# The opening of a two-layer trunk on one core: modulation tiles shared out anew, x loaded in halves, squares added by VectorE, gate dots one place later

## What is computed

```python
m  = (silu(c)     @ w_mod[i] + b_mod[i]).reshape(Bsz, 1, 9, 1024)      # latents
mc = (silu(c_ctx) @ w_mod[i] + b_mod[i]).reshape(1, 1, 9, 1024)        # context
def _modulate(h, g, m, k):
    return rms_norm(h, g) * (1 + m[:, :, 3*k + 1]) + m[:, :, 3*k]
def _half_ffn(h, g, m, k, w1, w3, w2):
    y = (silu(_modulate(h,g,m,k) @ w1) * (_modulate(h,g,m,k) @ w3)) @ w2
    return h + 0.5 * m[:, :, 3*k + 2] * y
# layer 0: half ffn -> attention | SSD -> half ffn; layer 1: half ffn -> RG-LRU | differential attention -> half ffn
```

## Time and profile before

| what | us |
|---|---|
| median of 3 runs (lowest, highest) | 2777.78 (2777.18, 2779.23) |
| the profiled execution, its own time | 2772.38 |
| its span, first to last instruction | 2770.5 |
| TensorE matmul busy in it | 2674.9 (97%) |
| VectorE busy | 2055.8 (74%) |
| ScalarE busy | 1172.4 (42%) |
| GpSimd busy | 390.4 (14%) |

### The profile page before, as it was taken

The page is one execution under the profiler, slowest core; times in us unless marked ns, Lnnn a source line. Parts: engine busy times, 40 slices in busy tenths (PEclk is TensorE's granted clock), DMA queues, the critical chain, the costliest instruction groups (busy, mean ns, idle before and its releaser), DMA issues.

```text
span 2770.5 us, 40128 instructions
## 1 busy us (share of the span) xinstructions
PE 2674.9 (97%) x15624; PEld 2513.8 (91%) x15624; DVE 2055.8 (74%) x3186; ACT 1172.4 (42%) x1855; POOL 390.4 (14%) x312
## 2 busy tenths in 40 slices
PE   5999999999998999999999999999999989999999
PEld 5999999998986799999999999999998875878998
DVE  7887878774558687877777878787888667666674
ACT  3233332446447644332323524232436867534342
POOL 3111111110012521111111211100011420211000
PEclk8999999999999999999999999999999999999999
DMA  9888989611120037889898479884522110378553
GB/s 346 213 236 244 281 251 272 156 65 61 54 68 2 1 123 201 240 240 266 243 268 223 138 214 252 240 240 135 166 76 82 54 61 1 114 197 236 154 163 126
DMA packets 161690, 464.13 MB, mean 168 GB/s; under 512 B 13280, under 2 KB 14432, under 8 KB 160608
## 3 DMA queue, kind: packets, MB, share of 16 engines
q1 hardware_dynamic: 87200, 247.65, 26.1%
q0 software_dynamic: 56448, 146.81, 24.4%
q10 hardware_dynamic: 17856, 67.12, 6.9%
HBM read 459.43 MB, written 148.90 MB: 220 GB/s over the span
## 4 chain that ended last, share of the span: by engine, by line
PE 81%; DVE 10%; DMA 4%; issue 2%; ACT 2%; POOL 0%; ACTq 0%; SPq 0%; DVEq 0%; POOLq 0%
PE banks L698 11%; PE banks L786 11%; PE banks L700 11%; PE banks L702 11%; PE banks L788 11%; PE banks L787 10%; PE banks L705 3%; PE banks L709 3%; PE banks L707 3%; DMA raw<-sums 2%; DVE banks L2028 1%; DVE tmp L2301 1%; PE banks L1233 1%; DVE wl L2023 1%; PE banks L1072 1%
## 5 line engine op out<-in xcount | busy, mean ns | idle before, releaser
L1372 ACT ACTIVATE wh<-raw 128x1024 fp32r<-128x1024 f32 (+2 forms) x194 | 181.7, 937 | 616.6 <-PE banks L702 459.9
L2028 DVE SCALAR_TENSOR_TENSOR banks<-mraw,scb 128x1024 f32<-128x1024 f32 x240 | 304.5, 1269 | 12.9 <-DMA mraw<-in_wmn 9.1
L2023 DVE TENSOR_TENSOR wl<-raw,wh 128x1024 fp32r<-128x1024 f32 (+2 forms) x216 | 234.8, 1087 | 93.5 <-ACT wh L1372 91.2
L1437 ACT ACTIVATE wh<-raw 128x512 fp32r<-128x512 f32 (+1 forms) x210 | 161.5, 774 | 320.9 <-DMA raw<-sums 153.8
L698 PE MATMUL banks<-hh,wh 128*128 128x384 f32 x1056 | 271.3, 338 | 9.9 <-DVE wl L2023 9.7
L700 PE MATMUL banks<-hl,wh 128*128 128x384 f32 x1056 | 270.0, 336 | 0.0
L702 PE MATMUL banks<-hh,wl 128*128 128x384 f32 x1056 | 269.8, 336 | 0.0
L786 PE MATMUL banks<-xh,wh 128*128 128x384 f32 (+1 forms) x796 | 258.5, 325 | 5.0 <-DVE wl L2095 4.8
L788 PE MATMUL banks<-xh,wl 128*128 128x384 f32 (+1 forms) x796 | 257.1, 323 | 0.0
L787 PE MATMUL banks<-xl,wh 128*128 128x384 f32 (+1 forms) x796 | 257.1, 323 | 0.0
L698 PE MATMUL banks<-xh,wh 128*128 128x384 f32 x880 | 231.1, 343 | 21.5 <-DVE xl L2293 12.1
(11 more groups left out here) (426 smaller groups left out, 6276.6 us busy)
## 6 DMA issues: line engine op xcount, KB each, us to landing
raw<-sums SPq DMA_DIRECT2D x140, 512.0 KB, 5.9
sums<-in_w POOLq DMA_DIRECT2D x88, 768.0 KB, 8.5
mraw<-in_wmn ACTq DMA_DIRECT2D x120, 512.0 KB, 5.3
a<-in_w SPq DMA_DIRECT2D x70, 512.0 KB, 4.3
sums<-in_w POOLq DMA_DIRECT2D x22, 1536.0 KB, 9.1
sums<-sums POOLq DMA_DIRECT2D x44, 768.0 KB, 9.5
raw<-in_w SPq DMA_DIRECT2D x80, 384.0 KB, 4.3
raw<-in_w SPq DMA_DIRECT2D x52, 512.0 KB, 3.7
```

The costliest lines, as they stand in the source:

```text
L1372: act.activation(wh[slot][:, 0:nk * P], raw[slot][:, 0:nk * P], ACT.Copy).then_inc(hi_done, 1)
L1437: act.activation(W_HI[slot_of(name, last)], W_SRC[name], ACT.Copy).then_inc(w_hi, 1)
L2023: dve.tensor_tensor(wl[slot][:, 0:nk * P], raw[slot][:, 0:nk * P], wh[slot][:, 0:nk * P].bitcast(F32), ALU.subtract).then_inc(lo_done, 1)
L2028: return dve.scalar_tensor_tensor(B67[:], tile, 1.0, scv[:, s, :], ALU.mult, ALU.mult, accum_out=out)
```

## The change

Tiles, loads and squares of the opening are dealt out anew, and three later places follow from it.

- TensorE takes eight mini tiles (8 to 11 of the scale, 0, 1, 4 and 5 of the shift), VectorE eight (12 to 15, and 2, 3, 6, 7). SP loads scale tiles first; the first two raw weight tiles come right behind `par`; `x` comes in two halves, each behind a group of mini tiles.
- The eight squares go to eight separate buffers (`squares`), VectorE adds them (seven additions, `add_square`), and TensorE sums `ssq` alone. GpSimd only waits for the last mini tile before it starts `weight_sums`.
- VectorE's dots on tiles 6 and 7 stand inside the first norm, behind the first four scaled chunks; the biases of the shift are added in two batches (`shift_batch`), on which ScalarE's `xh` waits.
- Gate tiles are loaded behind the weights of up-chunk 1 (`load_gate_minis`), their dots use `scb0` and stand one place later: behind chunk 0, ahead of and behind chunk 1, ahead of chunk 2. ScalarE's Silu of `scb` moves to up-chunk 1.
- The two `mraw` tiles of up-chunk 2 move to the down places j = 5 of rounds 1 and 2, which then have two tiles each.

```diff
-PE_MINI = (1, 3, 5, 7, 9, 11, 13)
-DVE_MINI = (0, 2, 4, 6, 8, 10, 12, 14, 15)
-MINI_GROUPS = ((0, 1, 2), (3, 4, 5, 6), (7, 8, 9, 10), (11, 12, 13), (14, 15))
+PE_MINI = (8, 9, 10, 11, 0, 1, 4, 5)
+DVE_MINI = (12, 13, 14, 15, 2, 3, 6, 7)
+MINI_GROUPS = ((8, 9, 12), (10, 11, 13), (14, 15), (0, 2), (1, 3), (4, 6), (5,), (7,))
...
         if f == 0:
-            place["down", 1, 2] = place["down", 2, 2] = 2
+            place["up", 2] = 0
+            place["down", 1, 2] = place["down", 2, 2] = place["down", 1, 5] = place["down", 2, 5] = 2
...
+        squares = [ssq, sq[0], sq[1], tmp[0], tmp[1], tmp[2], tmp[3], rstd]
...
+                        if (f, g, i) == (0, 0, 1):
+                            load_gate_minis()
...
+            def load_gate_minis():
+                for q in range(2):
+                    sp.wait_ge(mini_mm, 2 + q)
+                    sp.wait_ge(mini_dot, (13, 18)[q])
+                    sp.dma_start(gmini[q][:], dr["wmn"][16 + 4 * q:20 + 4 * q].rearrange("t p n -> p t n")).then_inc(gmini_landed, 16)
...
             def norm_sums(n, segs):
                 pe.wait_ge(ssq_acc, 7 * (n + 1))
+                if n == 0:
+                    for a, b, _s in segs:
+                        mm = pe.matmul(NP[:, a:b], cst("ones"), ssq[:, a:b], start=True, stop=True)
+                    mm.then_inc(norm_sum, 1)
+                    return
...
             for j in PE_MINI:
-                if j == 11:
-                    pe.wait_ge(con_landed, 16)
+                if j == 0:
+                    pe.wait_ge(x_landed[0], 32)
                     norm_sums(0, SEGS)
-
+                if j == 4:
+                    pe.wait_ge(rstd_ready, 1)
...
-                        if 0 < f < 3 and ch == 1:
-                            take_scb(f + 2, scb)
+                        if f < 3 and ch == 1:
+                            take_scb(f + 2 if f else 1, scb)
...
+            act.wait_ge(par_landed, 16)
+            act.activation(sc[:].rearrange("p k s -> p (k s)"), pr("cc"), ACT.Silu).then_inc(sc_ready, 1)
+            split_hi(0, 0, 0, KC)
+            split_hi(1, 1, 0, KC)
             act.wait_ge(scb_landed, 16)
             act.activation(scb0[:], scb0[:], ACT.Silu).then_inc(scb_ready, 1)
-            act.wait_ge(par_landed, 16)
-            act.activation(sc[:].rearrange("p k s -> p (k s)"), pr("cc"), ACT.Silu).then_inc(sc_ready, 1)
-            act.wait_ge(x_landed, 16)
             for j in range(KC):
-                square(j, 0, x[:, j, :], T)
-            split_hi(0, 0, 0, KC)
-            split_hi(1, 1, 0, KC)
-            act.wait_ge(eps_set, 1)
+                if j % 4 == 0:
+                    act.wait_ge(x_landed[j // 4], (32, 16)[j // 4])
+                act.activation(squares[j][:], x[:, j, :], ACT.Square).then_inc(sq_done, 1)
             norm(0, SEGS, lambda j: None)
             load_scb(scb)
-            take_scb(1, scb)
             ffn(0, KC, 1, T, T)
...
                         def ahead():
+                            if f == 0 and 1 <= ch < 3:
+                                gate_dots(2 * ch - 1)
+                            if f < 3:
+                                dot_mods(f, ("up", ch))
+
+                        def behind():
                             if f == 0 and ch < 2:
                                 gate_dots(2 * ch)
-                            if f < 3:
-                                dot_mods(f, ("up", ch))
-
-                        def behind():
-                            if f == 0 and ch < 2:
-                                gate_dots(2 * ch + 1)
                             if ch >= 2:
...
+            def add_square(j):
+                dve.wait_ge(sq_done, j + 1)
+                if j > 1:
+                    dve.wait_ge(ssq_acc, j - 1)
+                dve.tensor_tensor(ssq[:], ssq[:], squares[j][:], ALU.add).then_inc(ssq_acc, 1)
...
+            def shift_batch(q):
+                dve.wait_ge(mini_mm, 2 + q)
+                dve.wait_ge(mini_dot, (12, 17)[q])
+                first_bias(4 * q, 2, 4).then_inc(mini_dot, 1)
+                dve.wait_ge(mini_dot, (13, 18)[q])
+
+            def first_between(q):
+                if q == 0:
+                    shift_batch(0)
+                    first_dots(6, 13)
+                    first_dots(7, 15)
+                if q == 1:
+                    shift_batch(1)
+
+            chain(dve.memset(eps[:], EPS))
+            split_lo(0, 0, KC)
+            split_lo(1, 1, KC)
+            dve.wait_ge(scb_ready, 1)
+            first_dots(12, 0)
+            for j in range(1, 4):
+                add_square(j)
+            first_dots(13, 2)
+            for j in range(4, KC):
+                add_square(j)
+            first_dots(14, 4)
+            first_dots(15, 6)
+            first_dots(2, 8)
+            first_dots(3, 10)
             dve.wait_ge(par_landed, 16)
             dve.wait_ge(mini_mm, 1)
...
             prep(0)
-            norm(0, SEGS, lambda s: None)
+            norm(0, SEGS, first_between)
...
-            add_squares(0, T)
+            pool.wait_ge(mini_landed[len(MINI_GROUPS) - 1], 16 * len(MINI_GROUPS[-1]))
```

More of the change, by code:

```diff
@@ L277, in pr @@
             return par[:, PCOL[n][0]:PCOL[n][1]]
-        mini = [at(f"mini{j}", [P, D], XH + j * D) for j in range(2 * KC)]
-        gmini = [at("gmini0", [P, 4, D], H + 4 * D), at("gmini1", [P, 4, D], H)]
+        mini = [at(f"mini{j}", [P, D], (H if j < KC else XH - KC * D) + j * D) for j in range(2 * KC)]
+        gmini = [at(f"gmini{q}", [P, 4, D], H + 4 * q * D) for q in range(2)]
+        squares = [ssq, sq[0], sq[1], tmp[0], tmp[1], tmp[2], tmp[3], rstd]
         scb0 = at("scb0", [P, 2, D], HID + 2 * HC * T - 3 * T)
@@ L504, in heads, with mini_out @@
             return col.unsqueeze(2).to_broadcast([P, n, width])
+        def mini_out(j, n=1):
+            bank = G[0][:, 0:512] if j >= KC else G[0][:, 512:1024] if j < 4 else NP
+            return bank[:, 2 * j:2 * (j + n)]
         def group(j):
@@ L2874, in _ @@
[L2874 to L2878 removed]
+            dve.wait_ge(mini_dot, 8)
+            chain(first_bias(KC, 4, KC))
             prep(0)
[L2880 removed]
+            norm(0, SEGS, first_between)
```

85 lines of the change are left out of this document (39 added, 46 removed).

## The result

The changed kernel takes 2793.45 us in the median of 6 runs (2783.3 to 2800.61), beside 2777.07 for the kernel before on the same chip: ratio 1.0057, 95% interval 1.0040 to 1.0073, so 16.4 us slower. Forecast were 2776.6 and a range up to 2781.0. The profiled execution took 2797.74, its span 2796.0, that is 25.5 us more than the profiled one of before; so this one trace loses some 9 us more than the medians do.

What follows compares the result with a forecast made beforehand. TensorE carries 81% of the chain but waits for VectorE's first `xl` in the opening. Terms -4.8 + 0.8 + 0.8 + 2.0 = -1.2 us, applied to the median, gave 2776.6, range 2772.5 to 2781.0.

Steps and rivals of the forecast that it cites:

- The steps on the start's instructions: Opening: VectorE delivers the first `xl` at 52.5 us, so the first feed-forward matmul starts there, not at 57.3: gain 4.8.
- dots at 1.36 throughout: Opening, VectorE: each dot takes 1.36 us, since GpSimd adds no squares; 2.66 was the far bound for two dots.
- The wait at the table load: Start of up-chunk 1: a table load of 1.28 between `wh` and Silu makes TensorE start later, loss 0.8 us.
- The gate dots: Chunks 0 to 2: moving VectorE's gate dots one place later costs nothing.
- Rival 2: Opening: TensorE also starts at full clock, saving 1.9 us; with rival 1 that is -5.9, 2771.9; chance 0.08.
- rival 4: Opening: the start is not gained because `x` in two halves lands 5 us later; +3.6, 2781.4; chance 0.06.
- Rival 1: Doubled down places: they are hidden by quicker loads or VectorE being ahead; -4.0, 2773.8; chance 0.22.
- the term for the down places j = 5: Rounds 1 and 2: the second tile delays VectorE's split of `A12`, so TensorE waits; loss 0.8 and 2.0 us.
- rival 3: Rounds 1 and 2: stream loads landing in 7.8 us, not 5.8, make it slower; +6.8, 2784.6; chance 0.06.
- ScalarE's wait for dots: Down places j = 5: `wh` for two weight splits waits behind the next load but is done in time, no cost.
- The other step that failed: After the start: the first matmul's gained time is gained for the whole program, unless a later stall gives it back.
- 6 us later weight sums are small: GpSimd's weight sums start at 37.3 us, not 31.6; 6 us are small, as round 1 reads them much later.

Runs made afterwards that it cites:

- a_nosums: The changed kernel without GpSimd's weight-sum transfers, input weights of the same size read instead: 4.1 us under `b_nosums` in the medians.
- b_nosums: The kernel before without GpSimd's weight-sum transfers, input weights of the same size read instead: 2758.8 us, ratio 0.9938.
- a_sums_early: The changed kernel with GpSimd's weight sums started earlier, at 30.37 us instead of 38.84: as slow as the changed kernel.
- a_late_start: The changed kernel with one dot on tile 7 made three more times, to start the first feed-forward product as late as before: ratio 1.0093, 0.36% over the changed kernel.
- b_rest: The kernel before with the new table of places, gate dots one place later on `scb0`, and table load moved to up-chunk 1: ratio 1.0038.
- b_sums_late: The kernel before with GpSimd's weight sums held until the first norm's sum over partitions, starting at 41.68 us: 0.2% faster (0.07 to 0.32).

## Why the prediction was wrong

The steps on the start's instructions held: first product at 53.25 against 52.5, dots at 1.36 throughout, VectorE without a gap, and 4.1 us gained there against 4.8. The wait at the table load held, 1.0 against 0.8, and there is no drain: the load begins 0.02 behind `wh` and Silu 0.01 behind the load. (The row that the prediction read this from couldn't show it: 3.08 us without work follow the load there.) The step left the clock out, though: with the 1.5 us that chunk 1 then takes longer the moved load costs 2.5. The gate dots cost nothing, as said. Rival 2 is out, the clock at the start was 0.50, and so is rival 4. Rival 1, the doubled places hidden for -4.0, is what the kernel would be without GpSimd's transfers, -4.1 in the medians; the sum agrees better than its terms.

**The step that failed is the term for the down places j = 5**, 0.8 + 2.0: it was mis-sized. The new table alone costs 0.37% (0.24 to 0.50), some 10 us, of which its trace puts 7.1 on the two places. In the changed kernel its two stretches lose 16. From the forecast -1.2 to the measured +16.4 are 17.6 us; this term is 4 to 8 of them, and the rest belongs to a second step, below. The mechanism of this term was the forecast one, down to the instruction: the second tile's load, the dots of j = 7 and ahead of `A12`, and TensorE waiting behind that split. Three things made the size wrong.

- I gave each load the median of before, 5.8. The loads at a doubled place are a chain of four, each issued on the dots of two tiles back; what counts is their sum, and it was 31.8 where I had 23.2. I had named this as rival 3 (each us beyond 5.8 counts twice in a round), but priced it for 7.8 us in both rounds, at +6.8, and gave it 0.06; four loads stood in the chain and not two; its remark on the weight sums' traffic was the right one. In round 1 the mean of the four was 7.96. The longest landing of before was 9.2, the DMA share 0.92: the spread was there to be read, and in this stretch the tail was the price.
- I costed TensorE's wait and not the clock behind it. Of the 11 us lost from 256 to 336, 7.7 are idle and 3.2 come from the granted clock (80 us at 0.96).
- I let ScalarE's wait for dots pass as harmless ("is done in that time"). It is so with loads of 3.7 us. With those of 6.7 it costs in round 1 the smaller of TensorE's two waits, 1.62 at 312.86, behind a `wh` held until 310.39; the 6.06 runs through loads and dots alone.

**The other step that failed** is the one that put everything behind the start at nothing: "whatever time that first matmul gains is gained for the whole program, unless a later stall gives it back". The later stalls are there. In the changed kernel 0.8 of the 4.1 is left at 86 us, and its trace loses another 9 behind 800 us, where TensorE waits 14.4 for pair splits in place of 3.8. Only with GpSimd's transfers: in `a_nosums` and `b_nosums` that wait is 0.

**The sentence that I would take back** is that 6 us later weight sums are small. They are, for their readers (SyncE waits for no sum in the changed kernel), and `a_sums_early` shows that their start isn't the loss. But it looked at who reads the sums, and the right question was what their traffic does to a place that has lost its slack.

**What stays open.** The full change stands at 1.0057, its rest without the opening at 1.0038, where the gained start asks for 1.0023. With the same start as before it is at 1.0093. So under GpSimd's transfers the new opening costs 9 us and more beyond its gain, and without them (`a_nosums`) nothing. The single profiles put some of it on the same two stretches, which lose 16 us in the changed kernel and in `a_late_start` by the milestones, and 12 in `b_rest`. More of it lies behind 800 us. From there to the end the ten profiles with the new opening and the sums fall back 9.5 us on average against the one of before (0 to 16), the seven others with the old opening 1.1 (-3 to 3); their waits for pair splits there are 6.8 to 19.3 us and 3.8 to 8.9. Without sums both kernels gain the same 11. The instructions there are the same, so what the opening hands on can only be timing, and it does harm only where GpSimd's transfers run; by what way is not shown. Neither the sums' start, nor the gate tiles' load, nor the order within GpSimd explains it. Between two such ratios the intervals leave some 6 us of room.

Of the versions that keep the weight sums, only `b_sums_late` beats both kernels, by 0.2% (0.07 to 0.32), and it is one start time that happens to be good. Its profiled execution was 2.8 us longer in span than that of before, so no trace shows the gain.

## What to carry to other kernels

A load that is issued on the completion of work two places back turns a doubled place into a chain of loads: cost it by the sum of the slow landings in that stretch, not by one median, and ask for the slack of the whole chain. Before an edit takes away slack in a stretch where the DMA engines are nearly full (0.92 here), take the competing traffic out once: if the edit then gains what its instruction times say, contention is the price. And follow a gain at the start further than its own stage: here 4.1 us were 0.8 some 30 us later, and part of the loss lay in stages that the edit left alone.

## What the runs showed of the hardware

- The spread of the times goes with the traffic. Without GpSimd's transfers five runs lie within 1.7 us (`b_nosums`) and 5.9 (`a_nosums`); with them the changed kernel's six span 17.3 (2783.3 to 2800.61) and 15 of the kernel before, beside those five, 15.5 (2771.14 to 2786.67).
- The sums' transfers cost the kernel before 17 us (0.9938), though GpSimd has 0% of its chain and SyncE waits for a sum only once, 0.4 us: they cost as traffic, not as a wait. The changed kernel's DMA share in 256 to 336 falls from 0.92 to 0.58 without them.
- After 6.06 us without work TensorE ran at half clock for about 5 us (323.33 to 328.3), 15 matmuls at 0.32 apiece. A wait of 1.62 us (at 312.86 in the changed kernel) left the clock at 1.00, one of 2.38 (at 75.09) was followed by 0.66 over 75 to 80. At this place all eleven profiles with the 2.38 have the drop, and none of the five with 1.42 or 1.43. The length of the wait alone doesn't tell: behind the same 1.6 us at about 605 the clock was 0.50 in `b_nosums` and 1.00 in `a_nosums`.
- The table load took 1.28 us and TensorE's wait grew by 1.0: no drain is to be seen on either side of it (`wh` ends at 72.82, the load runs from 72.84 to 74.12, Silu starts at 74.13).
